# Mixture-of-experts stages of a three-layer kernel: rounds of one or two experts over four column groups instead of two or four experts at once

## The reference

```python
logit_g = (h @ w_rg + b_rg).astype(F32)
grp = jnp.argmax(logit_g, axis=-1)
...
top_v, top_i = lax.top_k(logit_e, TOP_K)                 # 2 experts of the group
gate = jax.nn.softmax(top_v, axis=-1) * p_grp
...
g, u = jnp.split(xb @ w_up[e], 2, axis=-1)               # 1024 -> 2 x 512
return (jax.nn.silu(g) * u) @ w_down[e]                  # 512 -> 1024
...
y = y[dest] * gate.reshape(-1)[order][:, None].astype(h.dtype)
return jax.ops.segment_sum(y, tok_sorted, num_segments=n_tok)
```

## Time and profile before

| | us |
|---|---|
| median of three runs | 1836.61 (1832.91 to 1839.12) |
| the profiled execution | 1836.74 |
| its span, first to last instruction | 1835.0 |
| TensorE busy | 1550.9 (85%) |
| VectorE, ScalarE busy | 453.4 (25%), 400.8 (22%) |
| mean granted clock of TensorE | 0.923 of 2.4 GHz |
| moved by DMA | 477.30 MB, 260 GB/s over the span |

### The profile page before, as it was taken

One profiled execution on the slowest core, in us unless ns is written; L12 is line 12 of the kernel. 1 busy time (PEld: TensorE's weight loads), 2 busy tenths in 40 slices (PEclk: granted clock), 3 DMA queues, 4 the chain that ended last, 5 costly groups with the idle time before them and its releaser, 6 DMA issues.

```text
span 1835.0 us, 20256 instructions
## 1 busy us (share of the span) xinstructions
PE 1550.9 (85%) x7433; PEld 705.2 (38%) x7434; DVE 453.4 (25%) x1278; ACT 400.8 (22%) x778; POOL 41.7 (2%) x80
## 2 busy tenths in 40 slices
PE   3999987889999999999979788777788887888674
PEld 2555444343333333333327444222226544332221
DVE  0103356432121212121222513111112523121111
ACT  1101224122222222222222412121212412222111
POOL 2000201000000000000000000000000000000000
PEclk9899969979999999999989888897999997998888
DMA  9857300229999999858582224999975321779995
GB/s 319 308 200 276 114 2 1 105 87 405 410 410 410 410 410 410 344 220 329 220 331 92 92 97 163 397 392 396 393 263 212 138 63 45 275 283 392 395 393 205
DMA packets 174249, 477.30 MB, mean 260 GB/s; under 512 B 8465, under 2 KB 18958, under 8 KB 174014
## 3 DMA queue, kind: packets, MB, share of 16 engines
q1 hardware_dynamic: 171136, 468.61, 66.9%
q0 software_dynamic: 2160, 6.51, 1.3%
q10 hardware_dynamic: 910, 1.59, 0.3%
HBM read 474.71 MB, written 1.97 MB: 260 GB/s over the span
## 4 chain that ended last, share of the span: by engine, by line
PE 66%; DMA 14%; DVE 8%; SPq 7%; issue 2%; ACT 2%; ACTq 0%; DVEq 0%; POOL 0%
PE psum L979 16%; DMA ring<-in_w_down 10%; PE psum L1006 9%; PE psum L929 6%; PE psum L941 6%; SPq L460 6%; PE psum L1638 5%; PE psum L662 5%; PE psum L1634 3%; DMA ring<-in_w_up 2%; PE psum L1208 2%; PE psum L1196 2%; SPq L467 1%; PE psum L542 1%; PE psum L1242 1%
## 5 line engine op out<-in xcount | busy, mean ns | idle before, releaser
L979 PE MATMUL psum<-ring,arena 128*32 128x512 f32 (+2 forms) x2304 | 413.0, 635 | 64.0 <-DMA ring<-in_w_up 62.0
L979 PEld LDWEIGHTS psum<-ring,arena 128*32 128x32 f32 (+2 forms) x2304 | 124.4, 128 | 343.5 <-issue 290.6
L1006 PE MATMUL psum<-ring,arena 128*32 128x512 f32 (+2 forms) x1152 | 211.4, 640 | 52.0 <-DMA ring<-in_w_down 43.3
L929 PE MATMUL psum<-arena 128*128 128x512 f32 x320 | 169.4, 635 | 3.2 <-DVE arena L1069 3.2
L1115 DVE TENSOR_TENSOR arena<-arena,psum 128x256 f32<-128x256 f32 (+1 forms) x37 | 20.4, 551 | 502.5 <-ACT arena L1045 502.5
L941 PE MATMUL psum<-xn,arena 128*128 128x512 f32 x296 | 133.3, 593 | 1.5 <-DVE arena L1090 1.5
L1006 PEld LDWEIGHTS psum<-ring,arena 128*32 128x32 f32 (+2 forms) x1152 | 59.1, 127 | 173.3 <-issue 106.8
L1045 ACT ACTIVATE arena<-psum 128x256 f32<-128x256 f32 (+1 forms) x37 | 18.0, 487 | 411.3 <-PE psum L979 411.3
L1638 PE MATMUL psum<-ring,hT 128*128 128x512 f32 x224 | 97.7, 593 | 0.0
L929 PEld LDWEIGHTS psum<-arena 128*128 128x128 f32 x320 | 54.2, 197 | 100.8 <-issue 95.2
L1067 DVE COPY arena<-psum 128x512 f32<-128x512 f32 x40 | 27.6, 691 | 252.2 <-PE psum L929 252.2
(11 more groups left out here) (329 smaller groups left out, 1441.6 us busy)
## 6 DMA issues: line engine op xcount, KB each, us to landing
ring<-in_w_expert_up SPq DMA_DIRECT2D x128, 1024.0 KB, 9.8
ring<-in_w_expert_down SPq DMA_DIRECT2D x64, 1024.0 KB, 12.2
ring<-in_w_gate SPq DMA_DIRECT2D x64, 1024.0 KB, 14.2
ring<-in_w_up SPq DMA_DIRECT2D x64, 1024.0 KB, 14.3
ring<-in_w_down SPq DMA_DIRECT2D x32, 2048.0 KB, 16.8
ring<-in_w_mod SPq DMA_DIRECT2D x12, 2048.0 KB, 14.6
ring<-in_w_in SPq DMA_DIRECT2D x6, 2048.0 KB, 9.1
ring<-in_w_out SPq DMA_DIRECT2D x6, 2048.0 KB, 13.4
```

Source lines behind the costliest of these rows:

```text
L929: return pe.matmul(ps[4 + 2 * t + n], comb[:, P * t:P * t + P], y_sb[:, 512 * n:512 * n + 512], start=False, stop=True, skip_group_check=True)
L979: mm = pe.matmul(out_, gotT[:, k, its], rhs, start=(k == 0), stop=(k == KD - 1))
L1006: mm = pe.matmul(ps[n][its, :], hidT[:, k, its], view[:, e, kk, 512 * n:512 * n + 512], start=(k == 0), stop=(k == chunks - 1))
```

## The change

**Places.** A round now has 32 places for each expert, in all stages, and takes one expert in block one and two in block two. The four column groups of TensorE no longer hold four experts but four parts of one expert's output (block one: a quarter of the 512 hidden columns, gate and up side by side, and a quarter of the 1024 output columns) or of two experts' (block two). An expert with more than 32 tokens takes an extra round for each further 32.

**Gather.** The gather is done for four experts at once, 32 places each, at the end of the last main round of the group before (`gather_group`), and comes out transposed (tokens as weights, marks as moving data), so that the eight transposes and two copies fall away. An extra round gathers again, for its own one or two experts (`sel_x`, `got_x`).

**Combine.** The result of a round is combined in the next round, in one piece between up and the wait for hid: 8 multiplies with 32 rows (block one) or 4 with 64 rows (block two), where before there were 4 with 128 rows.

**Ring.** 12 slots of 8 KB per partition; an expert's six loads of 1 MB each fill six of them. In block two the gate and up weights of an expert come in one load each, 8 KB in a row for each partition, where before a load took 2 KB of each of four experts. Other weights take two slots at once.

**Loop.** One turn is a group of four experts, so the code of four (or two) main and extra rounds stands in it. At the end of each main round TensorE waits for its own down (`w_y`) before it frees the last slot.

```diff
-SLOT = 4096
-RING = 6
+SLOT = 2048
+RING = 12
+ROUND = 6
...
+GROUP = 4
+W = 32
...
+        def expert_loads(sp, plan, sources):
+            base, turns, rounds = plan.n, sources[0].shape[0], len(sources) // ROUND
+            slots, _ = plan.loop(turns, len(sources))
             with sp.Fori(0, turns) as turn:
+                for j, (src, (slot, sem, _)) in enumerate(zip(sources, slots)):
+                    sp.wait_ge(sems["piece_used"], turn * len(sources) + (base + j - RING + 1))
+                    src = src[bass.ds(turn, 1)][0]
+                    dst = ring[:, slot, :]
+                    if len(src.shape) == 3:
+                        dst = dst.rearrange("p (k n) -> p k n", k=src.shape[1])
+                    sp.dma_start(dst, src).then_inc(sem, 16)
...
+        def second_sources(layer):
+            gate, up = (ins[n][layer].rearrange("g (b e) (p k) n -> e (g b) p (k n)", e=GROUP, p=P)
+                        for n in ("w_gate_2", "w_up_2"))
+            down = ins["w_down_2"][layer].rearrange("g (b e) (k p) n -> e (g b) p k n", e=GROUP, p=P)
+            out = []
+            for e in range(0, GROUP, 2):
+                out += [gate[e], up[e], gate[e + 1], up[e + 1], down[e], down[e + 1]]
+            return out
...
+        def each_round(eng, at, which, extra_round, main_round):
+            rounds = GROUP // experts_of(which)
             eng.wait_ge(*at("ranked"))
+            with eng.Fori(0, NE // GROUP) as turn:
+                for i in range(rounds):
+                    n = eng.value_load(extra[0:1, bass.ds(turn * rounds + i, 1)], min_val=0, max_val=7)
+                    begin = extra_round(turn, i, None)
                     with eng.If(n > 0):
+                        if begin:
+                            begin()
                         with eng.Fori(0, n):
...
+            def gather(select, width, out):
+                for k in range(KD):
+                    for t in range(NT):
+                        mm = pe.matmul(out(k)[:, 0:width], xn[:, t, P * k:P * k + P], select[:, t, 0:width],
+                                       start=(t == 0), stop=(t == NT - 1))
+                    if k == KD // 2 - 1:
+                        first = mm
+                return first, mm
+            def gather_group():
+                pe.reg_add(groups, groups, 1)
+                g = pe.snap(groups)
+                pe.wait_ge(sems["w_sel"], g)
+                first, mm = gather(sel, P, lambda k: G[k // 4][:, P * (k % 4):P * (k % 4) + P])
+                first.then_inc(sems["w_g0"], 1)
+                mm.then_inc(sems["w_g1"], 1)
...
+            def combine():
+                w, wide = W * at_once, S * at_once
+                for t in range(NT):
+                    for n in range(P // w):
+                        r = slice(w * n, w * n + w)
+                        out_ = ps[4 + n][:, S * t:S * t + S] if which == 1 else ps[4 + 2 * t + n]
+                        mm = pe.matmul(out_, comb[r, P * t:P * t + P], y_sb[r, 0:wide], start=False, stop=True,
+                                       skip_group_check=True)
+                return mm
...
+            def up(turn, i, got, col, main):
+                out_ = lambda j: U[quadrant(j), 0:2 * P].rearrange("p (u n) -> p u n", u=2)
+                if which == 1:
+                    for piece in range(4):
+                        w = slot_ready(turn, ROUND * i + piece).rearrange("p (k u q n) -> p k u q n", k=2, u=2, q=4)
+                        for kk in range(2):
+                            k = 2 * piece + kk
+                            for j in range(4):
+                                mm = pe.matmul(out_(j), got[:, k, col:col + W], w[:, kk, :, j, :],
+                                               start=(k == 0), stop=(k == KD - 1))
+                        if main and piece < 3:
+                            mm.then_inc(sems["piece_used"], 1)
+                else:
+                    for piece in range(4):
+                        slot_ready(turn, ROUND * i + piece)
+                    first = slots[ROUND * i][0]
+                    for k in range(KD):
+                        for j in range(4):
+                            e, half = j // 2, j % 2
+                            w = ring[:, first + 2 * e:first + 2 * e + 2, S * k + P * half:S * k + P * half + P]
+                            mm = pe.matmul(out_(j), got[:, k, col + W * e:col + W * e + W], w,
+                                           start=(k == 0), stop=(k == KD - 1))
+                mm.then_inc(sems["w_up"], 1)
+            def down(turn, i, main):
+                for piece in range(2):
+                    w = slot_ready(turn, ROUND * i + 4 + piece).rearrange("p (k n) -> p k n", k=2)
+                    if which == 1:
+                        for kk in range(2):
+                            k = 2 * piece + kk
+                            for j in range(4):
+                                mm = pe.matmul(Y[quadrant(j), 0:S], hidT[:, W * k:W * k + W], w[:, kk, S * j:S * j + S],
+                                               start=(k == 0), stop=(k == 3))
+                    else:
+                        for half in range(2):
+                            for n in range(2):
+                                j = 2 * n + piece
+                                src = 2 * piece + half
+                                mm = pe.matmul(Y[quadrant(j), :], hidT[:, W * src:W * src + W], w[:, half, 512 * n:512 * n + 512],
+                                               start=(half == 0), stop=(half == 1))
+                    if main and piece == 0:
+                        mm.then_inc(sems["piece_used"], 1)
+                mm.then_inc(sems["w_y"], 1)
...
+            def combine_turn(gates, col):
+                for t in range(NT):
+                    w = W * at_once
+                    for o in range(0, P, w):
+                        mm = pe.matmul(U[o:o + w, S + P * t:S + P * t + P], gates[:, t, col:col + w], ident,
+                                       start=True, stop=True)
+                mm.then_inc(sems["w_ct"], 1)
+            def round_(turn, i, got, gates, col, main, ready):
                 pe.reg_add(win, win, 1)
                 v = pe.snap(win)
...
+                combine_turn(gates, col)
+                if ready:
+                    pe.wait_ge(sems[ready[0]], ready[1])
+                up(turn, i, got, col, main)
+                pe.wait_ge(sems["w_ysb"], v + part)
+                combine()
+                if main and i == rounds - 1:
+                    gather_group()
                 pe.wait_ge(sems["w_hid"], v)
+                pe.transpose(U[:, 0:P], hid, ident).then_inc(sems["w_ht"], 1)
+                if main:
+                    pe.sem_inc(sems["piece_used"], 1 if which == 1 else 4)
+                pe.wait_ge(sems["w_hsb"], v)
+                down(turn, i, main)
+                if main:
+                    pe.wait_ge(sems["w_y"], v)
                     pe.sem_inc(sems["piece_used"], 1)
...
+                        pe.wait_ge(sems["w_xg_v"], g)
+                        pe.wait_ge(sems["w_xg_s"], g)
+                    return
+                pe.reg_add(extras, extras, 1)
+                x = pe.snap(extras)
+                width = W * at_once
+                pe.wait_ge(sems["w_selx"], x)
+                _, mm = gather(sel_x, width, lambda k: G[1][:, width * k:width * k + width])
+                mm.then_inc(sems["w_gx"], 1)
+                pe.wait_ge(sems["w_selgx"], x)
+                round_(turn, i, got_x, sel_gate_x, 0, False, ("w_xgx", x))
+            def main_round(turn, i):
+                round_(turn, i, gotT, sel_gate, W * at_once * i, True, None)
...
+            def scaled(dst, src, k0, n, wide):
+                by = scale[:, k0:k0 + n].unsqueeze(2).broadcast_to([P, n, wide])
+                ins_ = dve.tensor_tensor(dst[:, k0:k0 + n, 0:wide], src.rearrange("p (k n) -> p k n", k=n), by, ALU.mult)
+                if shift is not None:
+                    current(ins_)
+                    ins_ = dve.tensor_tensor(dst[:, k0:k0 + n, 0:wide], dst[:, k0:k0 + n, 0:wide],
+                                             shift[:, k0:k0 + n, 0:1].broadcast_to([P, n, wide]), ALU.add)
...
+                dve.reg_add(extras, extras, 1)
+                x = dve.snap(extras)
+                dve.wait_ge(sems["w_cur"], dve.snap(currents))
+                current(dve.tensor_scalar(it[:, 0:NT, :], it[:, 0:NT, :], -float(W), None, ALU.add))
+                marks(sel_x[:, :, 0:width], it, at_once).then_inc(sems["w_selx"], 1)
+                dve.wait_ge(sems["w_selx"], x)
+                gates(sel_gate_x[:, :, 0:width], sel_x[:, :, 0:width], it, at_once).then_inc(sems["w_selgx"], 1)
+                dve.wait_ge(sems["w_gx"], x)
+                scaled(got_x, G[1][:, 0:KD * width], 0, KD, width).then_inc(sems["w_xgx"], 1)
```

(32 more changed lines are left out.)

405 lines of the change are left out of this document (156 added, 249 removed).

## The result

The changed kernel takes 1990.35 us (median of 4 runs, 1980.29 to 1997.77) against 1837.2 us: a ratio of 1.0833, 95% interval 1.0781 to 1.0886. The prediction, 1850 us in a range of 1820 to 1880, was wrong. The profiled execution, the slowest of the four, has a span of 1996.0 us.

The account below looks back on a forecast made before the run. Block one: TensorE and queues full, TensorE setting the pace; block two: TensorE waits for weights. Block one -3.6, block two's layers 0 and +13.1, clock +4: 13.5 us on 1836.7, so 1850 us, range 1820 to 1880.

Parts of the forecast that it names:

- Rival (3): Loop over four experts, 2463 TensorE instructions, doesn't stay loaded: 1852 to 1870 us; chance of over 5 us 0.07.
- the prediction's own signs of being wrong: Under 400 GB/s before 740 us, rounds off by over 0.5 us, a 3.5 us combine, well over 50 instruction packets.
- The price of a block: Fetching TensorE code: each 16 KB instruction packet was put at about 1 us.
- The cover: Loop over four experts: load-paced turns hide ten refetched blocks; the last two turns pay 2 us, or 20.
- The rule of the page: TensorE's store holds 2048 instructions; a jump to a page outside may wait for a load: at least 2 us.
- forecast -3.6: Block one: residual starts at 942 us instead of 945.7, a gain of 3.6 us.
- the residuals of block two: Block two's expert stages: layer one gains 0, layer two loses 13.1 us.
- the clock's 4 us: Block two: array work behind each layer's last load takes 2 us more at clock 0.83, 4 in all.
- the combine: In each round: 1.8 us if row groups overlap, 3.5 if not; taken as 1.8 plus 0.2 for the switch.
- the gap at a main round's end: TensorE's new wait at a main round's end (drain, count, loop's end, first load): 2.0 us.
- a main round: Sum of a main round's parts: 10.6 us in block one, 11.45 in block two.
- an extra round behind another: Extra round with its own gather and scaling: 13.1 us in block one, 13.5 in block two.

Follow-up runs that it names:

- 'pairs': Changed kernel, complete, with block one's loop over two experts a turn instead of four and gathers of two (64 places): 1847.21 us (1.0073).
- experiment 3: Kernel before, TensorE's block one loop written out twice (1364 instructions): 1834.9 us; four times (2726): 1878.03 us.
- experiment 4: Changed kernel without block one's nine extra rounds and their code, its TensorE loop there written out twice (2233 instructions): 1784.47 us (0.9737).
- experiment 7: Block one of 'pairs' with block two's stages of before, plus 64 gather places an expert in block one: 1838.07 to 1925.25 us in six runs.
- experiment 1: Changed kernel without block one's nine extra rounds: their code kept but skipped, 1886.96 us; their code taken out, 1787.74 us.
- experiment 6: Block one of 'pairs' with block two of before: 1836.65 us; kernel before with block two's gate and up as one piece per expert: 1870.28 us.

## Why the prediction was wrong

The step that failed is code loading, which the sum has at nothing. Rival (3) gave the reasons, and two of its sentences are wrong: that the packets of a turn's ten blocks, "about 1 us each", are what they cost, and that "the load-paced turns hide them". It put 2 to 20 us on them, with a chance of 0.07 of over 5; the runs show 144.8 us (the changed kernel's residual against that of 'pairs'). Two of the prediction's own signs of being wrong stand in the profile: 331 GB/s before 740 us, and 118 instruction packets.

- **The price of a block.** The 1 us was the length of the packet, and the packet is as long as before. But the branch waits from the moment it is taken until the block is there: 6.1 to 7.5 us at most in each of five kernels (changed, same work without extra rounds, experiments 3, 4 and 7), against 0.2 for a branch whose target is loaded. I took a transfer's duration for its latency.
- **The cover.** A turn of four experts has 61.4 us of loads. At full clock TensorE needs 4 x 9.3 + 3.8 = 41 us of it. The stalls (220.7 us in front of TensorE's work in 39 waits, less 1.5 in each of the 31 that stand at a round's start, over about 8 turns: some 22 a turn) would by themselves nearly have fitted: 63. But the clock was low as well, 0.78, and up took mostly 5.3 to 6.1 us instead of 3.64: 41 + 22 + 4 x 2 = 71, and turns of 74 were measured (hid's transposes at 399.46 and 473.48). Above 61.4 the loads wait, and all of it counts: 8 x 12.6 = 101, near the 96.8 of experiment 1, where the loads set the pace to the end. In the changed kernel the loss up to expert 23's transpose of hid is 96.5 us too (835.83 against 739.31 in 'pairs'), but in six turns, with expert 16's extra round no longer hidden; that the two numbers agree is chance. From there on TensorE paces, every stall counts in full, and the last transpose has lost another 48.3 (1085.68 against 940.85, less the 96.5). How much of all this is stalls and how much the clock was not separated: in 'pairs' too the clock was below full (0.91), and many an up took 5.2 us.
- **The rule of the page.** The Trainium skill ("Runtime: NRT & Kernel Launch", Instruction fetch mechanics) says that a taken branch whose target isn't in "the current 2-page window" forces a fetch before execution goes on. These runs bear out the wait: branches of 6.1 us in experiments 3 and 4. They don't bear out two pages: a page is 256 instructions there, and in 'pairs' the jump back over some 1270 took 0.23 us at most. I had quoted the rule and then priced it by the packet.
- **Most of the rest held.** There were 79 transposes of hid, as counted. In 'pairs', where code costs nothing, block one ends at 945.38, 0.3 us earlier than before (forecast -3.6); the residuals of block two start at 1379.87 and 1829.31, which adds 0.6 (0) and 12.1 (13.1), the clock's 4 us included: 1847 us, 14.0 over before where 13.5 was forecast. That it comes so near is partly luck, since errors cancel: the combine took 1.15 us (L971), not 2.0, and the gap at a main round's end 1.55, not 2.0, so a main round is 9.3 us and not 10.6; against it, an extra round behind another lasts 13.2 to 13.7 us (13.1), with up at a lower clock in many (5.2 us), and 'pairs' has eight gathers more. One row was also read loosely: the earlier trace rows shows a packet of q14 and none of q8, the queue of the 29, so it is q8 alone that was idle there.
- **The combine.** Sixteen records of 256 columns on 32 rows each took 1.15 us, where one after the other was priced at 3.5: the four row groups work at once. The Trainium skill's factor of 3.07 ("TensorE: Matmul & The Clock Gate", Measured speedup vs the span model, for 512 columns) had given an estimate of 1.14; this trace agrees.

So without code loading the change is what was forecast, a small loss: what TensorE saves in block one's rounds goes to the extra rounds, and layer two's extra rounds are the loss. The other 144 us are code loading, with the low clock that goes with its gaps.

## What to carry to other kernels

Count the instructions that one turn of a loop passes through, short skipped stretches included, before unrolling it or adding a rarely used branch: here up to 1270 on TensorE stayed loaded, 1791 came and went in the one profile taken, 2233 and more were fetched again each turn. A long stretch that is always jumped over cost one wait of 5 us in the first turn and nothing later. Price a skip or a jump back in a loop that doesn't fit at 6 us, not at the length of the packet: of the skips of 331 instructions 19 of 32 waited, of those of 169 in experiment 3 only 8 of 30. And where the clock is low between the stalls, cover that is computed at full clock is too wide.

## What the runs showed of the hardware that was not expected

- A branch of TensorE to a block not loaded mostly takes 5 to 6.7 us, once 7.5; its packet of 16 KB takes about 1.1 of them.
- Loops of nearly the same length (2463 instructions, and 2464 by the order or some 2390 by the trace) cost 144 us or about 7, by whether the code is passed through.
- 38 blocks fetched again in straight code cost nothing; only the jumps back waited, 6.1 us each.
- Six runs of the program whose loop passes through 1791 instructions took 1838 to 1925 us, where the kernel before varies by 6 us.
- Block two's weights, gate and up with 8 KB in a row, came at 417 to 418 GB/s in the changed kernel, with 2 KB at 394; block one's, with 4 KB, at 409 to 410. That the row length makes the difference is not shown (experiment 6).
